# Order of the products within a weight tile: all 512-column matmuls of a call, then all its 256-column ones

## What is computed

```python
proj = h @ w_in[l]
...
y_a = (y_a * jax.nn.silu(z_a)) @ p_a[l]
...
o = m @ w_out[l]
...
proj = h @ w_in
...
return out @ w_out
...
h = h + jnp.square(jax.nn.relu(hn @ ffn_w1[i])) @ ffn_w2[i]
gate = jax.nn.sigmoid(rms_norm_2(h, norm_ple[i]) @ ple_w_gate[i])
```

## Time and profile before

| what | us |
|---|---|
| median of three runs | 2211.44 |
| lowest, highest | 2207.67, 2222.29 |
| span of the profiled execution | 2208.4 |
| TensorE busy in it | 2165.8 |
| VectorE busy | 1576.6 |
| ScalarE busy | 1107.4 |
| GpSimd busy | 109.3 |

### The profile page before, as it was taken

How to read it: one execution, slowest core, us unless ns; L and a number is a source line. 1 busy time by engine, 2 the same in 40 slices (tenths; PEclk the granted TensorE clock), 3 DMA queues, 4 the chain that set the end, 5 groups by cost and what they waited for, 6 DMA issues and landing times.

```text
span 2208.4 us, 40905 instructions
## 1 busy us (share of the span) xinstructions
PE 2165.8 (98%) x15336; PEld 1884.0 (85%) x15336; DVE 1576.6 (71%) x2398; ACT 1107.4 (50%) x1749; POOL 109.3 (5%) x96
## 2 busy tenths in 40 slices
PE   6999999999999999999999999999999999999997
PEld 5998888888888888888888888888888888888887
DVE  6985877888887577687666667675666566567867
ACT  3444544555554465465455445554444454445454
POOL 0000000000000010210000003000000000000203
PEclk8999999999999999999999999999999999999999
DMA  9995455455544577565543345556565656555552
GB/s 364 404 375 184 161 182 165 152 172 163 172 158 163 178 251 243 179 201 191 188 138 130 127 143 191 182 171 208 171 208 184 195 174 204 183 194 182 184 187 94
DMA packets 116273, 424.88 MB, mean 192 GB/s; under 512 B 13232, under 2 KB 13616, under 8 KB 115888
## 3 DMA queue, kind: packets, MB, share of 16 engines
q1 hardware_dynamic: 111744, 406.61, 54.6%
q0 software_dynamic: 4400, 16.45, 2.2%
HBM read 414.62 MB, written 8.39 MB: 192 GB/s over the span
## 4 chain that ended last, share of the span: by engine, by line
PE 91%; DVE 5%; ACT 2%; issue 1%; DMA 0%; SPq 0%; DVEq 0%; ACTq 0%
PE ps L2186 46%; PE ps L2187 23%; PE ps L2293 5%; PE ps L2562 3%; PE ps L2235 1%; PE ps L2237 1%; PE ps L2236 1%; PE ps L2563 1%; DVE acc L1342 1%; DVE wlo L1311 1%; PE ps L2715 1%; ACT whi L725 1%; DMA xt<-in_x 0%; PE ps L2218 0%; PE ps L2259 0%
## 5 line engine op out<-in xcount | busy, mean ns | idle before, releaser
L2186 PE MATMUL ps<-acts,whi 128*128 128x512 f32 x3312 | 1196.5, 403 | 3.0 <-DVE wt L1317 1.7
L1311 DVE TENSOR_TENSOR wlo<-raw,whi 128x1024 fp32r<-128x1024 f32 x629 | 787.2, 1267 | 433.1 <-ACT whi L725 430.7
L725 ACT ACTIVATE whi<-raw 128x1024 fp32r<-128x1024 f32 x671 | 703.5, 1057 | 650.3 <-PE ps L2187 566.4
L2187 PE MATMUL ps<-acts,wlo 128*128 128x256 f32 x3312 | 927.8, 280 | 0.0
L2186 PEld LDWEIGHTS ps<-acts,whi 128*128 128x128 f32 x3312 | 620.9, 187 | 155.7 <-issue 7.5
L2187 PEld LDWEIGHTS ps<-acts,wlo 128*128 128x128 f32 x3312 | 625.8, 189 | 4.6 <-issue 3.4
L2186 PE MATMUL ps<-hidn,whi 128*128 128x512 f32 x1280 | 447.5, 393 | 2.2 <-DVE s L1317 1.7
L2187 PE MATMUL ps<-hidn,wlo 128*128 128x256 f32 x1280 | 358.4, 280 | 0.0
L2186 PEld LDWEIGHTS ps<-hidn,whi 128*128 128x128 f32 x1280 | 239.5, 187 | 57.2 <-DVE wlo L1311 3.6
L2187 PEld LDWEIGHTS ps<-hidn,wlo 128*128 128x128 f32 x1280 | 241.9, 189 | 0.5 <-issue 0.5
L725 ACT ACTIVATE half<-ps 128x256 f32<-128x256 f32 (+1 forms) x335 | 126.0, 382 | 64.3 <-PE ps L2187 49.7
(11 more groups left out here) (341 smaller groups left out, 2008.1 us busy)
## 6 DMA issues: line engine op xcount, KB each, us to landing
raw<-in_stream SPq DMA_DIRECT2D x767, 512.0 KB, 4.2
gate_dram<-stage POOLq DMA_DIRECT2D x32, 128.0 KB, 2.5
gab<-gate_dram POOLq DMA_DIRECT2D x8, 512.0 KB, 5.1
xt<-in_x SPq DMA_DIRECT2D x1, 2048.0 KB, 9.5
xt<-in_x POOLq DMA_DIRECT2D x1, 2048.0 KB, 8.5
ple_dram<-pr__111 POOLq DMA_DIRECT2D x4, 512.0 KB, 3.7
pj<-ple_dram POOLq DMA_DIRECT2D x1, 2048.0 KB, 11.5
out<-y__143 SPq DMA_DIRECT2D x2, 512.0 KB, 2.8
```

Source lines behind the costliest of these rows:

```text
L725: return nc.scalar.activation(dst, src, ACT.Copy)
L1311: tt(wlo[:, n % SPLIT, :], raw[:, in_stream(g) % RAW, :], whi[:, n % SPLIT, :].bitcast(F32), ALU.subtract).then_inc(raw_used, 1)
L2186: mm(ps[bank + n][:, :], whi[:, n0 % SPLIT, c:c + P], act[:, off + kt + k, :], start=kt + k == 0, stop=False)
L2187: ins = mm(ps[bank + n][:, 0:T], wlo[:, n0 % SPLIT, c:c + P], act[:, off + kt + k, 0:T], start=False, stop=kt + k == last)
```

## The change

In `use` the loop over the banks is run twice. The first pass issues the 512-column products of all banks of the call, each bank's wait on `evac_done` among them, and the second pass issues all 256-column products, with the increment of `quarters` behind each bank's last.

```diff
                 for n in part:
                     if kt == 0 and evac is not None:
                         pe.wait_ge(evac_done, evac[0] + (evac[1] + n + 1))
                     for k in range(2):
                         c = k * 512 + n * P
                         mm(ps[bank + n][:, :], whi[:, n0 % SPLIT, c:c + P], act[:, off + kt + k, :], start=kt + k == 0, stop=False)
+                for n in part:
+                    for k in range(2):
+                        c = k * 512 + n * P
                         ins = mm(ps[bank + n][:, 0:T], wlo[:, n0 % SPLIT, c:c + P], act[:, off + kt + k, 0:T], start=False,
                                  stop=kt + k == last)
                     ins.then_inc(quarters, 1)
```

## The result

| | us |
|---|---|
| changed kernel, median of four runs | 2233.91 (2232.91 to 2234.30) |
| before, the four runs beside it | 2209.56 (2207.57, 2207.67, 2211.44, 2222.29) |
| ratio, 95% interval | 1.0098 (1.0068 to 1.0129) |
| span of the profiled execution, before and after | 2208.4, 2231.2 |

The change makes the kernel 1% slower: 22.8 us in the profiled spans. The forecast was 2229. One of the four times of before lies 10.9 us and more above the rest; the experiments show that this is no accident.

What follows compares the result with a forecast made beforehand. TensorE, busy 98% of the span, was taken to pace the kernel by how closely matmuls follow each other. 2208.4 + 21.2 (waits) - 4 (spacing) = 2225.6 us span, 2229 us as median; range 2196 to 2250.

Steps and rivals of the forecast that it cites:

- The boundary wait: At 38 clean block boundaries (FFN, PLE gate, output projection), bank 0 evacuated late: 0.54 us each, 20.5 us.
- 0.7: Three boundaries that wait already (KV's end, two in the opening): a little later after the change, 0.7 us together.
- Banks 1 to 3: Behind a delayed boundary these banks do not wait again; additions 0.42 us apart, margins 0.12 and 0.16 us.
- The spacing: Matmuls behind their like: tile sum unchanged in the FFN, some time back in the stages outside FFN and PLE, -4 us.
- The sign set for it: A tile lasting under 2.70 or over 2.80 us would show the spacing term wrong.
- rival B: Slower: 0.230 us after any 512, 0.120 after any 256; 11.4 us lost, nothing back, 2244 us; chance 0.20.
- A: Faster: a 512 behind a 512 limited by its columns alone, 0.214 us; 49.5 us gained, 2183 us; chance 0.10.
- C: Slower: WO's dearer pace, 0.006 us more a pair, spreads into FFN and PLE; 13 us, 2246 us; chance 0.12.
- D: The wait doesn't appear, or the cold first 512 costs less: 2207 to 2215 us; chance 0.08.

Runs made afterwards that it cites:

- mirrored: Each bank issued as 512, 256, 256, 512 in place of the changed kernel's grouping by kind: 2210.95 us, ratio 0.9942 to the kernel before.

## Why the prediction was right, and where its terms were off

**The boundary wait.** The mechanism, its place and the number of places held: no wait for bank 0 at full FFN, PLE and WO boundaries before, one at each after, none new in WB, NG and NO. The forecast was 0.46 late and 0.08 lost behind it, 0.54; measured 0.38 and 0.10 in the FFN, and 0.50 in the mean over the 38. The 1.16 us from the last matmul to the addition's end was right. What was too large was the 0.14 from that end to the matmul, taken from a REST boundary: the chain in the FFN has 0.04 there. 38 x 0.50 + 0.7 = 19.7 us against 21.2. The last tile in the old order takes 19.7 us off the changed kernel's 2233.9, and its 256s put first take 20.3 off the 2233.5 beside it. Bank 0 completed first leaves 9.6 over the first of these (2223.8 - 2214.2) where 9 to 11 were worked out from its lead.

**Banks 1 to 3.** They didn't wait again, as said. The reason given had a wrong number: copies behind each other start 0.27 apart ((1.21 - 0.39) / 3) and additions 0.33, not 0.42; the margins were larger than stated.

**The spacing.** This is the step that was off. I took that a tile keeps its sum in the FFN and gains 4 us before it. The sign set for it, a tile of over 2.80 us, was too wide to catch what came. In the FFN a grouped tile takes 0.02 us more than the alternating one of the first profile: 2.793 against 2.773 by starts. Over the 280 tiles of FFN and PLE that is 5.6 us, the spacing of rival B: a 512 keeps 0.230 behind its like, and the 256s lie at 0.119. What remains of the 22.8 is 22.8 - 19.7 - 5.6 = -2.5 us before the FFN; the forecast had -4. The starts bear this out: the FFN's seventh tile starts at 1409.32 before and at 1409.45 after, so what the waits ahead of it cost, 3 x 0.60 + 0.7 = 2.5, came back almost whole. In WO, where the alternating tiles were in their dearer pace in that execution, it is 32 x (2.830 - 2.793) = 1.2 us; the rest lies mostly in the WB stage, where no run tells what it is. So 17.2 was forecast for a sum that came to 22.8, and the terms' errors were -1.5, +5.6 and +1.5. The 2229 was 5 us low.

**Rivals.** A (a 512 behind a 512 at its columns alone, 0.214) is refuted: 0.229 to 0.230 in every grouped kernel, 512s in runs of 8 and 16. Its 0.214 was half the 0.429 between records of L2715; that each of those is two passes over its columns no run shows. Nor do the runs show, for this operand format and with a load for every matmul, the gap that the Trainium skill gives in "TensorE: Matmul & The Clock Gate", section on the back-to-back issue gap, for isolated matmuls, 216 and 109 ns: it is 230 and 119 to 120 here. B was right as to the FFN's spacing and wrong in giving nothing back elsewhere. C named something real, that the WO stage's pace can stand in the FFN, but laid it on the wrong kernel: it is the kernel before that falls into it, the changed one doesn't. D is refuted, the wait stands 38 times. The rule of the Trainium skill that banks should rotate, so that evacuation overlaps the next group's matmuls ("Perfetto Trace Analysis", section on optimizing Tensor performance, Matmuls), is borne out with a price: 0.50 us for a boundary at which the evacuation is no longer covered.

**What I did not foresee.** Before's time is two-valued. The forecast leaned on one profiled execution of the faster kind. Had it been of the other kind, the same reasoning with 0.353 a pair would have had to decide whether the grouped order inherits that pace, and a median of 2234 would be 0.5% slower, not 1%. The two ratios, 1.0098 and 1.0046, are both right for the mixture of paces beside which they were measured. That the first came out near the forecast is in this part luck: three of the four runs of before beside it were of the faster kind, as the profiled one was, and of the 46 later ones only 7.

## What to carry to other kernels

When the order within a tile is changed, look at which instruction signals the consumers and how far it now stands from the point where its buffer is asked for again: here 2.20 us of lead became 0.84 against a need of 1.2, and that alone cost 0.9%, while the same grouping with the signal early cost nothing like it. Before a difference of half a per cent is explained, run the old kernel ten times and compare a steady stretch, by instructions per microsecond, in two of its profiles. Of the orders tried, completing each bank in turn (512, 512, 256, 256) keeps the signals early and the pace steady.

## What the runs showed of the hardware

Strictly alternating 512- and 256-column matmuls, each with its own load, ran at 0.347 us a pair in some stretches and at 0.353 in others, at a granted clock of 1.00 in both. The FFN, in which TensorE does not stop, kept one of them throughout in each of two profiled executions, a different one in each; of 46 runs of the kernel before beside the experiments, 7 were near 2210 and 39 near 2225. Orders in which like follows like had one pace each: 2.793 us a tile grouped by four banks, 2.807 by two, 2.787 bank by bank or mirrored. The cause of the two paces stays open. The same instructions at the same addresses ran at both, and where TensorE stopped at every block boundary the pace changed from block to block, never inside an FFN block; that the moment of the restart decides is a guess and not shown. A first 512 behind a wait was followed by the next 0.10 to 0.12 us later than otherwise, on top of the wait.
